# Who adds the scaled residual ahead of two layer norms: TensorE through a scaled identity, or VectorE

## What is computed

```
x = layer_norm(ALPHA * x + mix, ln1_g[layer], ln1_b[layer])   # mix = [attention, memory attention] @ w_out
ffn = conv_ffn(x, ...)
x = layer_norm(ALPHA * x + ffn, ln2_g[layer], ln2_b[layer])
```

## Time and profile before

| | us |
|---|---|
| median of 3 runs | 930.18 (929.97 to 930.19) |
| the profiled execution, its own time | 931.36 |
| its span, first to last instruction | 929.6 |
| TensorE busy | 896.1 (96%) |
| VectorE busy | 651.3 (70%) |
| ScalarE busy | 488.9 (53%) |
| mean granted TensorE clock | 0.988 |

### The profile page before, as it was taken

The page is one execution under the profiler, slowest core; times in us unless marked ns, Lnnn a source line. Parts: engine busy times, 40 slices in busy tenths (PEclk is TensorE's granted clock), DMA queues, the critical chain, the costliest instruction groups (busy, mean ns, idle before and its releaser), DMA issues.

```text
span 929.6 us, 14619 instructions
## 1 busy us (share of the span) xinstructions
PE 896.1 (96%) x5650; PEld 770.5 (83%) x5650; DVE 651.3 (70%) x1182; ACT 488.9 (53%) x890; POOL 41.6 (4%) x73
## 2 busy tenths in 40 slices
PE   8999999799999899999999999998999999999997
PEld 8898988688978788677888888887997788888885
DVE  5769686755767547768788676786755778678676
ACT  5464375555765447544554544544655355454541
POOL 2005000100001100000000000000000100000000
PEclk9999999999999899999999999999999999999999
DMA  8845434364373662212565566545342365655561
GB/s 307 306 160 156 157 121 154 125 232 158 95 201 132 237 204 70 69 47 91 204 204 183 186 198 197 185 162 204 128 167 92 137 203 205 199 184 185 184 200 45
DMA packets 45504, 155.06 MB, mean 167 GB/s; under 512 B 5404, under 2 KB 8060, under 8 KB 45436
## 3 DMA queue, kind: packets, MB, share of 16 engines
q1 hardware_dynamic: 40688, 141.78, 45.6%
q10 hardware_dynamic: 4748, 12.36, 4.3%
HBM read 152.78 MB, written 1.34 MB: 166 GB/s over the span
## 4 chain that ended last, share of the span: by engine, by line
PE 85%; DVE 9%; ACT 3%; issue 1%; DMA 1%; POOL 1%; DVEq 0%; ACTq 0%; SPq 0%
PE ps L2012 16%; PE ps L2027 13%; PE ps L765 8%; PE ps L2011 7%; PE ps L658 6%; PE ps L660 5%; PE ps L659 5%; PE ps L675 3%; PE ps L676 3%; PE ps L677 3%; PE ps L845 3%; DVE wlo L626 3%; PE ps L897 2%; PE ps L854 2%; PE ps L777 2%
## 5 line engine op out<-in xcount | busy, mean ns | idle before, releaser
L626 DVE TENSOR_TENSOR wlo<-raw,whi 128x1024 fp32r<-128x1024 f32 (+1 forms) x263 | 314.3, 1218 | 31.0 <-ACT whi L620 30.5
L620 ACT ACTIVATE whi<-raw 128x1024 fp32r<-128x1024 f32 (+1 forms) x263 | 271.5, 1047 | 103.0 <-DMA raw<-in_ws 40.2
L2012 PE MATMUL ps<-t,whi 128*128 128x512 f32 x640 | 221.7, 396 | 0.0
L2011 PE MATMUL ps<-t,wlo 128*128 128x256 f32 x560 | 156.2, 279 | 0.0
L658 PE MATMUL ps<-t,whi 128*128 128x256 f32 (+1 forms) x480 | 139.9, 291 | 0.3 <-ACT arena L1642 0.3
L659 PE MATMUL ps<-t,whi 128*128 128x256 f32 (+1 forms) x480 | 136.5, 284 | 0.0
L660 PE MATMUL ps<-t,wlo 128*128 128x256 f32 (+1 forms) x480 | 136.4, 284 | 0.0
L2012 PEld LDWEIGHTS ps<-t,whi 128*128 128x128 f32 x640 | 115.9, 188 | 22.5
L2011 PEld LDWEIGHTS ps<-t,wlo 128*128 128x128 f32 x560 | 105.6, 189 | 3.5
L2027 PE MATMUL ps<-whi,r 128*128 128x512 f32 x352 | 98.0, 390 | 0.0
L658 PEld LDWEIGHTS ps<-t,whi 128*128 128x128 f32 (+1 forms) x480 | 92.3, 192 | 6.5 <-issue 3.9
(11 more groups left out here) (268 smaller groups left out, 1276.5 us busy)
## 6 DMA issues: line engine op xcount, KB each, us to landing
raw<-in_ws SPq DMA_DIRECT2D x256, 512.0 KB, 4.2
vecs<-in_vecs ACTq DMA_DIRECT2D x12, 512.0 KB, 6.2
arena<-in_ws ACTq DMA_DIRECT2D x5, 512.0 KB, 5.3
raw<-in_ws SPq DMA_DIRECT2D x4, 384.0 KB, 3.3
tb<-brow ACTq DMA_DIRECT2D x8, 192.0 KB, 5.8
rows<-in_mem SPq DMA_DIRECT2D x2, 512.0 KB, 4.0
x<-in_x SPq DMA_DIRECT2D x1, 1024.0 KB, 9.9
rows<-in_ws ACTq DMA_DIRECT2D x2, 512.0 KB, 7.4
```

The costliest lines, as they stand in the source:

```text
L620: a.i.activation(whi[:, j % NSPLIT, 0:n], raw[:, j % NRAW, 0:n], ACT.Copy).then_inc(*a.sig("hi", u))
L626: d.i.tensor_tensor(wlo[:, j % NSPLIT, 0:n], raw[:, j % NRAW, 0:n], whi[:, j % NSPLIT, 0:n].bitcast(F), ALU.subtract).then_inc(*d.sig("lo" ...
L2011: p.i.matmul(ps[:, b, 0:T], wl[:, k, :], thi[:, k, :], start=False, stop=False)
L2012: mm = p.i.matmul(ps[:, b, :], wh[:, k, :], t2[:, k, :], start=k == 0, stop=k == 7)
```

## The change

In the lists the steps ("add_x", "a", 0), ("add_x", "a", 1), ("add_x", "b", 0) and ("add_x", "b", 1) go. The first output product of each half starts the sums. In dve_layer_norm of these two layers VectorE computes rows = ALPHA * x + sums for each half before bn_stats, which reads rows, as does the pass that subtracts the mean. The feed-forward layers (f0, f1) keep their products with the scaled identity.

```diff
-        ("fin", m1), ("turn", n1, 0), ("turn", n1, 1), ("log", n3), ("cmp",), ("turn", n2, 0), ("add_x", "a", 0), ("add_x", "a", 1),
+        ("fin", m1), ("turn", n1, 0), ("turn", n1, 1), ("log", n3), ("cmp",), ("turn", n2, 0), 
...
-        ("turn", g4, 0), ("turn", g4, 1), ("tile", "b_q", 5), ("log", g5), ("add_x", "b", 0), ("proj", "b", 0, 0), ("val", g4),
-        ("add_x", "b", 1), ("fin", g4), ("log", g6), ("mul", g5), ("proj", "b", 1, 0), ("proj", "b", 0, 1), ("proj", "b", 1, 1),
+        ("turn", g4, 0), ("turn", g4, 1), ("tile", "b_q", 5), ("log", g5), ("proj", "b", 0, 0), ("val", g4),
+        ("fin", g4), ("log", g6), ("mul", g5), ("proj", "b", 1, 0), ("proj", "b", 0, 1), ("proj", "b", 1, 1),
...
-                p.fill(2 * q + z, ("gained", POST[s], q, z))
+                p.fill(2 * q + z, ("gained", POST[s], q, z) if s in POST else ("summed", s, q, z))
...
+        by_rows_ = s in ("a", "b")
         for n in range(2):
             d.wait_ge(*done[n])
-            d.i.bn_stats(bn[:, n, :], ps[:, 2 * q + n, :]).then_inc(*d.sig("dve"))
+            if by_rows_:
+                d.i.scalar_tensor_tensor(rows[:, q, half[n]], x[:, q, half[n]], ALPHA, ps[:, 2 * q + n, :], ALU.mult, ALU.add
+                                         ).then_inc(*d.sig("summed", s, q, n))
+                d.wait_ge("summed", s, q, n)
+            d.i.bn_stats(bn[:, n, :], rows[:, q, half[n]] if by_rows_ else ps[:, 2 * q + n, :]).then_inc(*d.sig("dve"))
...
-            d.i.scalar_tensor_tensor(rows[:, q, half[n]], ps[:, 2 * q + n, :], ag[:, 0:1], vec(gname)[:, half[n]],
+            d.i.scalar_tensor_tensor(rows[:, q, half[n]], rows[:, q, half[n]] if by_rows_ else ps[:, 2 * q + n, :], ag[:, 0:1], vec(gname)[:, half[n]],
                                      ALU.subtract, ALU.mult).then_inc(*d.sig("normed", s, q, n))
...
-            elif what == "add_x":
-                pe_add_x(p, "a", a[1], "normed", "a")
             elif what == "proj":
-                pe_project(p, *a, True)
+                pe_project(p, *a, False)
```

More of the change, by code:

```diff
@@ L2166, in pe_moba @@
                 pe_val(p, *a)
-            elif what == "add_x":
-                pe_add_x(p, "b", a[1], "normed", "b")
             elif what == "proj":
-                pe_project(p, *a, True)
+                pe_project(p, *a, False)
     def act_moba(a):
```

## The result

| | before | after |
|---|---|---|
| median of 12 runs each, us | 929.97 (928.11 to 931.45) | 932.97 (930.90 to 934.54) |
| ratio, 95% interval | | 1.0034 (1.0023 to 1.0044) |
| profiled execution: time, span, us | 931.36, 929.6 | 932.17, 930.4 |
| TensorE, VectorE busy, us | 896.1, 651.3 | 890.1, 655.9 |
| mean granted TensorE clock | 0.988 | 0.989 |

The change costs 0.34%, 2.1 to 4.1 us. 931.9 had been forecast. The experiments show that one of the forecast's terms was right only for some executions. Two timed runs of the later batches lie far off all others, 2248.41 us (the kernel before, beside e1 to e4) and 1256.51 us (e5), and the ratios leave them out.

A forecast was written before the change was run, and what follows sets the result against it. TensorE, holding 85% of the chain, was taken as the bound. Sparse +0.6 (3.0 lost, 2.4 gained) and block +1.06 (2.36 lost, 1.3 gained) made +1.7: 933.1 profiled, 931.9 us median, range 930.9 to 932.9, wide range 928.5 to 934.5.

The forecast's parts named there:

- 8.96 us on the chain: Sparse and block layers: the eight removed products' time on the chain that ended last, 5.13 + 1.91 + 1.92 us.
- Part 1, sparse gain: Sparse layer: removing the products gains 2.4 us, out of bounds of 1.7 and 5.13, as TensorE then waits for pc.
- Whether the low clock stays costs nothing here, as this wait covers it: Sparse layer, before cmpt 0: TensorE's wait until 383.05 hides low clock in the first output product and log n4.
- Part 2, block gain: Block layer: removing 3.83 us of products gains 0.7 + 0.6 = 1.3 us, out of bounds of 0.7 and 3.83.
- Part 3, the norms: Four layer norms: VectorE's sums take 2.88 us to bn_aggr; first norms grow by 1.45 us, second by 1.55.
- That sources cost the same: Normalizing pass in the norms: reading sums from SBUF instead of PSUM was priced at nothing (746 and 745 ns).
- Who waits: Behind the norms: TensorE waits for x and the fourth weight piece, losing 3.0 us (sparse) and 2.36 (block).
- the wide range: Whole kernel: 928.5 to 934.5 us, from between B and C up over the single low-clock stretch of rival A.
- rival A: TensorE's clock: new idle stretches bring low clock; one uncovered stretch costs 1.7 us (933.6), two 3.4 (935.3); chance 0.26.
- 1.18 us taken off: Whole kernel: subtracted to go from the profiled execution's 931.36 us to the median of the runs shown, 930.18.
- B: Whole kernel: TensorE bounds throughout, 8.96 us go and the tails take 5.4 back: -3.6, 926.6 us; chance 0.14.
- C: Norms and block layer: cheaper sums (0.7 less) and more block gain (0.7): +0.3 us, 930.5 us; chance 0.17.

The follow-up runs named there:

- e1: The kernel before with the eight residual products of the sparse and block layers left out and nothing in their place: 927.32 us, ratio 0.9981.
- e4: The kernel before, norms untouched, with the residual's products moved as halves into the changed kernel's TensorE waits, both layers: 928.45 us, ratio 1.0001.
- e5: The changed kernel with the block layer put back, so the change is in the sparse layer alone: 931.84 us, ratio 1.0030.
- e6: The changed kernel with the sparse layer put back, so the change is in the block layer alone: 930.88 us, ratio 1.0016.
- e7: The kernel before, unchanged, profiled a second time: 929.69 us.
- e2: The changed kernel with the removed products put back, so the residual is added twice: 935.13 us, ratio 1.0068 to the kernel before.
- e10: The kernel before, unchanged, profiled a third time: 928.24 us.
- e11: The kernel before, unchanged, profiled a fourth time: 929.24 us.
- e9: The kernel before with the residual's products moved into the changed kernel's TensorE waits in the sparse layer alone: 928.79 us, ratio 1.0007.
- e3: The changed kernel with VectorE's split of the fourth weight piece moved ahead of the second norm's sums: 933.27 us, ratio 1.0046 to the kernel before.
- e8: The changed kernel, unchanged, profiled a second time: 932.12 us.

## Why the prediction came out as it did

**What bounds the kernel.** Read rightly in kind: VectorE took TensorE's place in the chain. But "8.96 us on the chain" was a poor measure of what could be gained.

**Part 1, sparse gain: the step that failed.** Forecast 2.4 us. In the trace it was made from, it is near: cmpt 0 2.64 (forecast 2.7), mul n3 2.03, ScalarE's copy 2.11, and the norm starts 2.07 earlier, counted from the first mask. But the sentence "Whether the low clock stays costs nothing here, as this wait covers it" asked the question only of the changed kernel. In the kernel before nothing covers it, so the drop costs that kernel 1.7 us (S 323.29 against 321.57). Of the six profiled executions with the sparse layer's products in this place, three had it (before, e6, e7) and three had not (e2, e10, e11). In e10 the norm starts 50.36 us behind the first mask, in the changed kernel 49.96: the gain is 0.4. I had put 3.5 us at the low level beside the row, worked out that they cost 1.7, and not carried that as a term which an execution has or has not.

**Part 2, block gain.** Right step by step: mask g6 0.72 (0.7), mul g5 0.74 (0.7), the wait before turn g5 1.60 (1.8), the copy 0.87 earlier (0.73), val g5 and the norm 1.26 (1.3).

**Part 3, the norms.** 2.76 us from first sum to bn_aggr in all four norms, 2.88 forecast. Single lines of the norm after, durations min/median/max in ns, against the earlier trace rows:

```profile
L1133 DVE SCALAR_TENSOR_TENSOR rows<-x,ps x8: 670/675/689, 426.4 to 737.5; 128x512 f32<-128x512 f32 x8
L1136 DVE BATCH_NORM_STATS2 stat<-rows x8: 694/695/695, 427.2 to 738.2; 128x6 f32<-128x512 f32 x8
L1136 DVE BATCH_NORM_STATS2 stat<-ps x8: 682/699/699, 618.2 to 924.2; 128x6 f32<-128x512 f32 x8
L1142 DVE SCALAR_TENSOR_TENSOR rows<-rows,stat,vecs x8: 744/748/752, 429.9 to 739.8; 128x512 f32<-128x512 f32 x8
L1142 DVE SCALAR_TENSOR_TENSOR rows<-ps,stat,vecs x8: 741/746/752, 619.9 to 925.8; 128x512 f32<-128x512 f32 x8
```

The new sum takes 675 ns, not 745: the 70 ns are the term's error. The price of the wait was right: 0.72 us from a sum to its bn_stats (427.16 - 426.44), 0.61 from bn_stats to the next sum, which waits for nothing of VectorE's: 0.11 us. The Trainium skill's "VectorE: DVE Perf Modes" (The DRAIN you can't avoid) has the semaphore at no extra cost in a chain of copies; these rows disagree by that 0.11. By an estimate from its fixed cost of 58 cycles for SBUF against 120 for PSUM (TRN2 errata section) the difference would be 65 ns; the last four rows show 4 ns for bn_stats and -2 ns for the normalizing pass. That sources cost the same held.

**Who waits.** Block layer: from the norm's start to the end 203.49 us against 201.13, 2.36 lost, as forecast (2.36). Sparse layer: from the norm's start to log g5 274.38 against 271.26 (before) and 271.21 (e10), 3.12 to 3.17 lost, 3.0 forecast. TensorE waits 2.11 us before T 7 0 where 1.9 were forecast, because a new gap of 0.36 us stands between bn_aggr and the pass in the first sparse norm (429.88); it is 0.67 from start to start, 0.31 before. The fourth pieces wait 1.35 and 1.16 us (1.5 and 1.6 forecast).

**Sum.** +1.7 forecast. By the traces: 2.1 (1.0 + 1.1) where the products meet the low clock, 3.9 (2.8 + 1.1) where they don't. The timed +3.0 (2.1 to 4.1) lies between, and the forecast +1.7 below it. That 932.97 still lies in the wide range owes something to luck: the range reached that far up for rival A, a drop in the changed kernel, which no profile of it shows behind cmpt 0. What the traces show is a drop that is missing in the kernel before. The 1.18 us taken off "for the median" hid the question: the profiled execution stood above the median, and its drop was worth 1.7. How often timed runs have the drop can't be read, since a run lists only its mean clock. E5 and e9 exclude the value that goes with a drop in every run of the kernel before, if their own runs pay nothing for one. The mean clocks hint that it is the rarer case: the two profiled executions of before with the drop have 0.988, the two without 0.989, and of the 64 timed runs of this kernel beside the experiments six list 0.988 or less. It is no more than a hint, as e6 had the drop at 0.991, with two other low stretches missing.

**The rivals.** A: no low stretch stands behind T 7 0 or T 10 0 in after, e3, e5, e6 or e8; the clock was 1.00 in every 4 us from 388 to 920. In the traces the clock decides the size in the kernel before and not in the changed one. For the timed runs this isn't shown: six of the changed kernel's twelve list a mean clock of 0.987 or less, where its two profiled executions have 0.989. The four at 0.987 took 932.9 us on average, no more than the four at 0.989 (933.1), as with a drop that a wait covers; the two at 0.986 took 934.5, and where their clock fell no trace shows. In e1 a drop behind cmpt 0 cost some 1.0 us. So a part of the +3.0 may be the clock's in the changed kernel. B and C are out: the main interval starts above both.

## What to carry to other kernels

A low-clock stretch in a profiled execution is a term that this execution has and others may not: before a gain is counted from idle time behind such a stretch, work out what the idle time is at full clock, and give both sums. Work put into a chain of short dependent steps is paid there nearly in full (3.2 and 2.4 us for four sums in each layer), while work taken from the busiest engine pays only as far as the next engine's input allows (in the sparse layer 0.4 of 3.4 us at full clock and 2.1 of 5.1 with the drop, in the block layer 1.3 of 3.8). To compare two traces, take distances between two steps on either side of the change.

## What the runs showed of the hardware

- The same kernel's low-clock stretches move from one execution to the next: near 176 to 188, 276 to 284 and 312 to 328 us in most profiles, none in the first two places in e6 and e9, and some 3.4 us at the 1.2 GHz level somewhere between 376 and 386 us in before, e1, e3, e6 and e7, none there in the others (e7 has 0.63 from 376 to 378 and 0.52 from 378 to 380: (0.37 + 0.48) x 2 x 2 = 3.4). E7 and e10 are the same kernel, one with it and one without; what decides is open.
- A scalar_tensor_tensor with a constant as its scalar (675 ns) was quicker than one with a scalar from a column of SBUF (745 ns), both 128x512 in fp32. Whether the scalar is the cause wasn't tried.
- GpSimd's two small operations (128x1) of the second sparse norm took 0.78 and 0.93 us in after, and as long in e2, e3, e5 and e8; in before, e1 and the others with the old norm they took 0.22 and 0.57. They run beside the normalizing pass, which now has both its inputs, the sums and the vector, in SBUF, where the sums came from PSUM. The timeline of GpSimd in the kernel after:

```profile
439.26 0.78 POOL L1081 TENSOR_SCALAR stat<-stat 128x1 f32<-128x1 f32 x1 [8.88 <-DVE stat L1138]
440.12 0.93 POOL L1084 TENSOR_TENSOR stat<-stat,nhalf 128x1 f32<-128x1 f32 x1
```

  The Trainium skill's "GPSIMD Engine Reference" (Specifications) says that GpSimd's way to SBUF is shared with VectorE, and contended by VectorE's operations with two inputs there. By that rule, the trace agrees. So do the first norms of after: the sparse layer's two operations start at 429.51 and 429.81, ahead of the pass (429.88), and take 0.22 and 0.57 us; the block layer's second one starts at 730.28, inside the pass (730.00), and takes 0.90. Spans on GpSimd are rough in this profile, but these repeat within 0.01 us. I had priced the pass's new source at nothing, and for VectorE that held; GpSimd's delay of 0.9 us was on the path in e3 alone.
- A gap of 0.36 us behind bn_aggr (0.67 us from start to start, where 0.31 is usual) came in the first sparse norm of after, e2, e3, e5 and e8, and not in the block layer; its cause is open.
